# The opening of a two-block transformer kernel: weights of the state-space scan prepared by matrix products, batched transposes, modulation blocks moved

## The reference, cut to what matters

```
h = rmsnorm(x, norm_mix)
dt = exp(log_dt);  ab = exp(lam * dt)                      # complex, per group and state
bb = (ab - 1) / lam * b                                    # complex, (group, state, channel)
bu = einsum('blgh,gph->blgp', h, bb)
xs[t] = ab * xs[t-1] + bu[t]                               # scan over the 256 tokens
y  = Re(einsum('blgp,ghp->blgh', xs, c)) + d_skip * h
a, g = split(gelu(y) @ w_glu);  x = x + a * sigmoid(g)
...
mod = silu(c) @ w_ada + b_ada                              # second block, 1024 -> 6144, two layers
```

## Time and profile before

| what | value |
|---|---|
| median of the runs | 2005.14 us |
| lowest and highest run | 2001.52 and 2005.61 us |
| span of the profiled execution, first to last instruction | 1998.3 us |
| TensorE busy | 1912.5 us (96% of the span) |
| VectorE, ScalarE, GpSimd busy | 934.3, 755.8, 1108.0 us |
| mean granted TensorE clock | 0.979 of full speed |
| first product with `w_glu` starts at | 124.61 us |

### The profile page before, as it was taken

The page is one execution under the profiler, slowest core; times in us unless marked ns, Lnnn a source line. Parts: engine busy times, 40 slices in busy tenths (PEclk is TensorE's granted clock), DMA queues, the critical chain, the costliest instruction groups (busy, mean ns, idle before and its releaser), DMA issues.

```text
span 1998.3 us, 31484 instructions
## 1 busy us (share of the span) xinstructions
PE 1912.5 (96%) x13077; PEld 1644.2 (82%) x13077; DVE 934.3 (47%) x1688; ACT 755.8 (38%) x1212; POOL 1108.0 (55%) x611
## 2 busy tenths in 40 slices
PE   8989999989999999899999999999999999989997
PEld 5578999878887788687778888888788988979997
DVE  7956641364935774732453111114386846372112
ACT  4343553332325422722323222222446435434443
POOL 6435997563535443343443444444468745757885
PEclk8999999989999999999999999999999999989999
DMA  6866776664122132124333323323634421655653
GB/s 165 239 215 225 256 230 219 239 216 156 62 76 64 33 126 64 32 64 137 127 107 126 95 79 121 104 63 110 209 116 128 159 85 54 204 196 174 189 173 98
DMA packets 289490, 276.60 MB, mean 138 GB/s; under 512 B 19802, under 2 KB 276324, under 8 KB 289092
## 3 DMA queue, kind: packets, MB, share of 16 engines
q1 hardware_dynamic: 286804, 271.42, 43.0%
q10 hardware_dynamic: 2192, 2.77, 0.4%
q0 software_dynamic: 352, 0.40, 0.1%
HBM read 266.70 MB, written 4.19 MB: 136 GB/s over the span
## 4 chain that ended last, share of the span: by engine, by line
PE 86%; DVE 6%; ACT 2%; POOL 2%; issue 2%; DMA 1%; SPq 1%; DVEq 0%; ACTq 0%; POOLq 0%
PE gb L2598 19%; PE gb L2599 18%; PE gb L2600 18%; PE gb L1757 3%; PE gb L1755 3%; PE gb L1756 3%; PE gb L1482 3%; PE gb L1483 3%; PE gb L1484 3%; POOL wl L2585 1%; PE mb L1208 1%; PE mb L667 1%; PE gb L667 1%; PE mb L1275 1%; DMA raw<-in_w_ada 1%
## 5 line engine op out<-in xcount | busy, mean ns | idle before, releaser
L2585 POOL TENSOR_TENSOR wl<-raw,wh 128x1024 fp32r<-128x1024 f32 (+3 forms) x448 | 977.8, 2201 | 797.0 <-ACT wh L819 796.7
L819 ACT CAST wh<-raw 128x1024 fp32r<-128x1024 f32 (+3 forms) x452 | 419.4, 937 | 680.8 <-PE gb L2600 399.7
L2598 PE MATMUL gb<-xh,wh 128*128 128x256 f32 (+1 forms) x1856 | 603.4, 325 | 11.0 <-DVE xl L1158 6.9
L2599 PE MATMUL gb<-xl,wh 128*128 128x256 f32 (+1 forms) x1856 | 599.5, 323 | 0.0
L2600 PE MATMUL gb<-xh,wl 128*128 128x256 f32 (+1 forms) x1856 | 599.4, 323 | 0.0
L2598 PEld LDWEIGHTS gb<-xh,wh 128*128 128x128 f32 x1856 | 351.8, 190 | 47.2 <-issue 14.6
L2600 PEld LDWEIGHTS gb<-xh,wl 128*128 128x128 f32 x1856 | 351.8, 190 | 27.6
L2599 PEld LDWEIGHTS gb<-xl,wh 128*128 128x128 f32 x1856 | 351.9, 190 | 27.2
L1755 PE MATMUL gb<-fhh,wh 128*128 128x512 f32 (+1 forms) x352 | 118.4, 336 | 0.0
L1757 PE MATMUL gb<-fhh,wl 128*128 128x512 f32 (+1 forms) x352 | 117.9, 335 | 0.0
L1756 PE MATMUL gb<-fhl,wh 128*128 128x512 f32 (+1 forms) x352 | 117.9, 335 | 0.0
(11 more groups left out here) (475 smaller groups left out, 3028.7 us busy)
## 6 DMA issues: line engine op xcount, KB each, us to landing
raw<-in_w_in SPq DMA_DIRECT2D x62, 1024.0 KB, 5.4
raw<-in_w_ada SPq DMA_DIRECT2D x48, 1024.0 KB, 5.5
raw<-in_w_ffn SPq DMA_DIRECT2D x44, 1024.0 KB, 5.2
raw<-in_mlp_w SPq DMA_DIRECT2D x32, 1024.0 KB, 5.6
raw<-in_w_ffn SPq DMA_DIRECT2D x16, 768.0 KB, 4.3
raw<-in_w_ffn SPq DMA_DIRECT2D x16, 640.0 KB, 4.1
raw<-in_ssm_w_glu SPq DMA_DIRECT2D x8, 1024.0 KB, 6.9
raw<-in_w_out SPq DMA_DIRECT2D x8, 1024.0 KB, 4.8
```

The lines of the kernel that those rows point to most:

```text
L819: nc.scalar.copy(split_half(wh, p, j, h), raw_half(p, it, j, h)).then_inc(hi_ready, 1)
L2585: nc.gpsimd.tensor_tensor(split_half(wl, p, j, h), raw_half(p, it, j, h), split_half(wh, p, j, h).bitcast(F32), ALU.subtract)\
L2598: nc.tensor.matmul(o, H[:, k, :], XH, start=st, stop=False)
L2599: nc.tensor.matmul(o, H[:, k, :], XL, start=False, stop=False)
```

## The change

What it does, by engine:

- Loads. C's real and imaginary parts come by two DMAs (256-byte runs) in place of sixteen; B comes by two DMAs from GpSimd's queue with each pair's 8 KB in one run (`Bq`), in place of four on SyncE's queue and two broadcasts of the gain `norm_mix`; the gain comes as 32 rows (`wq`). SyncE no longer waits for the three lambda loads ahead of its other loads. Some buffers move to other places: x by chunk goes to the ring's slots, so that the first ring load waits for `xg` in place of the transposes of U; the zeros for the Toeplitz matrix wait for these transposes, and the copy of V waits for the zeros.
- B. GpSimd makes diagonal matrices of the gain (`wdiag`); TensorE multiplies B with them (64 products), which transposes it and weights it; VectorE reads the result in PSUM for `Bb`, and its own product with the gain goes.
- C. 32 products with a strided identity take the place of 8 transposes, and come ahead of U. ScalarE copies `Ct` between the fourth and the fifth of its eight `xg` copies.
- x is transposed in two halves through two PSUM banks, after U, then the vectors, `warm(3, 2)`, and only then the two products for `fac`. `warm(21, 3)` becomes `warm(3, 2)`. ScalarE copies all four row-zero parts of F ahead of `fac`.
- V. Transposes, copy and products go by two pairs at a time (16 steps in place of 32). Modulation blocks 0 to 7 stand behind steps 1, 2, 3, 6, 7, 8, 10, 11, blocks 8 and 9 ahead of step 12; k_products(0) stands in step 9, the skip products and k_back(0) in step 11. Behind the last step come k_products(1), block 10, k_back(1), block 11, `warm(8, 1)`. Blocks 12 and 13 stand behind d = 3 and d = 5 of the y loop.
- The ring has 12 modulation blocks, then two `w_glu` blocks, so that the Toeplitz copies (ahead of ring load 12) are issued ahead of the `w_glu` blocks.
- E. GpSimd makes seven halves and the chunk powers in between; VectorE makes one (`e_beside(3, 1)`). `e_last` and `gate_lo` go; GpSimd makes the low parts of the first two `w_glu` blocks.
- The place of U's product with `fac` in VectorE's own order (behind the root, ahead of `f_group(1)`) is the same in both kernels.

The diff, cut to its core:

```diff
-        EARLY_ADA, EARLY_GLU = 10, 2
+        EARLY_ADA, EARLY_GLU = 12, 2
+        K_FIRST = 9
...
             if g == 0:
-                sp.wait_ge(s_U, 1)
+                sp.wait_ge(s_xg, CH)
...
+            for j in range(4):
+                x_by_group(j)
+            act.wait_ge(s_ct5, 1)
+            act.wait_ge(s_vz, 2)
+            nc.scalar.copy(Ct[:, 0, :, 0:GH], gb[:, 1, :].rearrange("p (q h) -> p q h", h=GH)).then_inc(s_Ctc, 1)
+            nc.scalar.mul(Ct[:, 1, :, 0:GH], gb[:, 2, :].rearrange("p (q h) -> p q h", h=GH), -1.0).then_inc(s_Ctc, 1)
+            for j in range(4, CH):
+                x_by_group(j)
...
+            for i in range(2):
+                act.wait_ge(s_xt, i + 1)
+                nc.scalar.copy(x[:, 4 * i:4 * i + 4, 0:SEQ],
+                               gb[:, 1:3, :].rearrange("p b (k t) -> p (b k) t", k=2)).then_inc(s_x1, 1)
...
+            for r in range(4):
+                f_row_zero(r)
+            act.wait_ge(s_fp5, 1)
+            nc.scalar.copy(fac[:, :], gb[:, 1, 0:NCH]).then_inc(s_fac, 1)
...
+            for b in range(PAIRS // 2):
+                act.wait_ge(s_w1t, b + 1)
+                if b >= 2:
+                    act.wait_ge(s_w1u, b - 1)
+                nc.scalar.copy(w1[:, 2 * (b % 2):2 * (b % 2) + 2, :, :],
+                               gb[:, 1 + b % 2, :].rearrange("p (a r m) -> p a r m", a=2, r=2)).then_inc(s_w1, 1)
...
-            warm(21, 3)
+            warm(3, 2)
+            pe.wait_ge(s_Bq, 16 * 2)
+            pe.wait_ge(s_gd, 1)
+            for ri in range(2):
+                for h in range(GH):
+                    for g in range(2):
+                        ins = nc.tensor.matmul(gb[64 * g:64 * g + 64, 3 * ri, PAIRS * h:PAIRS * h + PAIRS],
+                                               Bq[:, ri, g, :, h], wdiag[:, g, h, :], start=True, stop=True)
+            ins.then_inc(s_Bt, 1)
+            pe.wait_ge(s_cnat, 16 * 2)
+            of_parity = ident.rearrange("p (q g h) -> p g q h", q=4, g=2)
+            for ri in range(2):
+                for r in range(8):
+                    for g in range(2):
+                        ins = nc.tensor.matmul(gb[64 * g:64 * g + 64, 1 + ri, 64 * r:64 * r + 64],
+                                               cnat[:, ri, r, :], of_parity[:, g, :, :], start=True, stop=True)
+            ins.then_inc(s_ct5, 1)
...
+            for b in range(PAIRS // 2 + 1):
+                if b == 12:
+                    for n in range(8, 10):
+                        ada_block(pe, n)
+                if b < PAIRS // 2:
+                    w1_transposes(b)
+                if b:
+                    v_products(b - 1)
+                if b in (1, 2, 3, 6, 7, 8, 10, 11):
+                    if b == 1:
+                        pe.wait_ge(s_sc, 1)
+                    ada_block(pe, (1, 2, 3, 6, 7, 8, 10, 11).index(b))
+                if b == K_FIRST:
+                    pe.wait_ge(s_Vc, 2)
+                    k_products(0)
+                if b == K_FIRST + 2:
+                    skip_products()
+                    k_back(0)
+            pe.wait_ge(s_w1, PAIRS // 2)
             k_products(1)
-            ada_block(pe, 5)
...
+            ada_block(pe, 10)
             k_back(1)
-            for n in range(7, EARLY_ADA):
-                ada_block(pe, n)
-            warm(7, 1)
+            ada_block(pe, 11)
+            warm(8, 1)
...
-                late = ((0,), (1,), (), (2,), (), (), (3,), ())[d]
+                late = ((), (), (), (0,), (), (1,), (), ())[d]
...
             dve.wait_ge(s_Ctc, 2)
-            e_beside(2, 1)
-            e_beside(3, 0)
+            e_beside(3, 1)
...
-            e_last(3, 1)
-            dve.sem_inc(s_E, 1)
```

More of the change, by code:

```diff
@@ L712, in _ @@
             sp.dma_start(lnat[:, 0, :], A["ssm_lam_re"][0].rearrange("(q g) p -> q (g p)", g=2)).then_inc(s_lnat, 16)
-            sp.wait_ge(s_lnat, 16 * 3)
             xc = A["x"][0].rearrange("(c j) d -> j c d", j=CH)
[L715 to L721, removed]
+            for ri, name in enumerate(("ssm_c_re", "ssm_c_im")):
+                sp.dma_start(cnat[:, ri, :, :], A[name][0].rearrange("(r g) h p -> (g h) r p", g=8)).then_inc(s_cnat, 16)
             for j in range(CH):
@@ L2336, in _, with x_by_group @@
             act.sem_inc(s_sin, 1)
-            for j in range(CH):
+            def x_by_group(j):
                 if j % 2 == 0:
@@ L2684, in _ @@
             ins.then_inc(s_U, 1)
-            pe.wait_ge(s_x1, 1)
+            pe.wait_ge(s_Ctc, 2)
+            pe.wait_ge(s_xnat, 16)
+            for i in range(2):
+                if i:
+                    pe.wait_ge(s_x1, 1)
+                for k in range(4):
+                    for a in range(2):
+                        ins = nc.tensor.transpose(gb[:, 1 + k // 2, (k % 2) * 256 + a * P:(k % 2) * 256 + a * P + P],
+                                                  xnat[:, a, (4 * i + k) * P:(4 * i + k) * P + P], ident)
+                ins.then_inc(s_xt, 1)
+            pe.wait_ge(s_vnat, 16 * NVEC)
+            pe.wait_ge(s_x1, 2)
+            for a in range(4):
+                ins = nc.tensor.transpose(gb[:, 1, a * P:a * P + P], vnat[:, a, :], ident)
+            ins.then_inc(s_vt, 1)
+            warm(3, 2)
+            pe.wait_ge(s_vc, 1)
+            pe.wait_ge(s_Bb, 1)
             pe.wait_ge(s_small, 32)
@@ L2688, in _ @@
             for a in range(2):
-                ins = nc.tensor.matmul(gb[:, 3, GH * a:GH * a + GH], const[:, REP:CHK], chk[:, a, :], start=True, stop=True)
+                ins = nc.tensor.matmul(gb[:, 1, GH * a:GH * a + GH], const[:, REP:CHK], chk[:, a, :], start=True, stop=True)
             ins.then_inc(s_fp5, 1)
-            pe.wait_ge(s_cnat, 16 * 8)
-            pe.wait_ge(s_gn, 16 * 8)
-            for ri in range(2):
-                for r in range(4):
-                    ins = nc.tensor.transpose(gb[:, 1 + ri, r * P:r * P + P], cnat[:, ri, r, :], ident)
@@ L2696, in _ @@
[L2696 to L2713 removed]
+            pe.wait_ge(s_fac, 1)
@@ new lines, in w1_transposes @@
+            def w1_transposes(b):
+                if b % 4 == 0:
+                    pe.wait_ge(s_F, b // 4 + 1)
+                    pe.wait_ge(s_F0, 2 * (b // 4 + 1))
+                if b >= 2:
+                    pe.wait_ge(s_w1, b - 1)
+                for e in range(2):
+                    q = 2 * b + e
+                    for ri in range(2):
+                        ins = nc.tensor.transpose(gb[:, 1 + b % 2, (2 * e + ri) * P:(2 * e + ri + 1) * P],
+                                                  Fg[q // 8][:, q % 8, ri, :, :], ident)
```

272 lines of the change are left out of this document (104 added, 168 removed).

## The result

| | before | after |
|---|---|---|
| median of the runs | 2005.38 us (2001.52 to 2006.93, 4 runs) | 2014.95 us (2011.33 to 2020.38, 4 runs) |
| ratio, 95% interval | 1 | 1.005 (1.0033 to 1.0068) |
| profiled span | 1998.3 us | 2009.5 us |
| U scaled | 40.8 | 47.2 |
| S starts | 76.6 | 92.2 |

What follows compares the result with a forecast made beforehand. TensorE, busy nearly throughout, bounds the kernel; only the first `w_glu` product's start shifts. U 2.9 us later, S 6.5 later, y 0.9 later, that product 2.6 earlier, plus 0.5 for the clock: -3.1, 2002 us. Range 1997 to 2010.

Steps and rivals of the forecast that it cites:

- B on TensorE: In the front, B's 64 products (128 instructions) take 4.5 us, bounds 3.5 and 11.6, ending at 13.5.
- the wait through ScalarE: In the front, behind C at 17.0, `Ct` copies (1.1) and four `xg` copies (3.8) hold U's transposes until 21.9.
- GpSimd's diagonal product (9.0): In the front, GpSimd's diagonal product, behind six DMA issues and some clears, is ready at 9.0, bounds 8.4 and 12.
- VectorE reaches `Bb` at 14.2: In the front, VectorE reaches `Bb` at 14.2, after B's products end at 13.5, so B's arrival costs nothing.
- V's start: Behind U, steps 0 to 7 and five blocks take 15.0; F(2), ready at 16.3, sets step 8.
- rival (a): Slower rival, low clock in B, C and V's start: U 8 us later, V 2 more, 2010 in all; chance 0.23.
- V's step: In V, a merged step of two pairs takes 1.25 us, bounds 1.15 and 1.46, in place of 1.46.
- What stands among the V products: Between U ready (43.7) and S's start (82.9), steps, blocks, K and skip products and V's copy take 39.1.
- The bound changes sides: Ahead of S, blocks and K products among V's products make TensorE the last instead of VectorE, by 9 us.
- The scan: S's scan on VectorE stays at 19.8 us, ready at 102.7; y starts at 102.8, the Toeplitz copies not last.
- The y loop: From y to the first `w_glu` product, eight steps of 2.4 make 19.2, without the 3.10 block wait, until 122.0.
- the two signs that the prediction named for being wrong: In the opening, S released by VectorE's own E work, or U ready before 40, would show the prediction wrong.

Runs made afterwards that it cites:

- experiment 4: `quiet`: kernel after, with GpSimd's last two clears and the two products of the skip gain moved behind `Bb`; 2016.79 us, ratio 1.0054 to the kernel before.
- experiment 6: `quiet_fac`: kernel of experiment 4 with the products for `fac` right behind U's transposes and their copy ahead of x's copies; 2023.02 us, ratio 1.0100 to the kernel before.
- experiment 1: Kernel after, with the low parts of the first two `w_glu` blocks back on VectorE; 2012.03 us, ratio 1.0039 to the kernel before.
- experiment 7: `fac_warm`: kernel of experiment 6 with three more warm products ahead of U's transposes; 2019.15 us, ratio 1.0078 to the kernel before.
- hold: Experiment 9: kernel of experiment 6 with GpSimd waiting for the end of the root before its E halves; 2013.09 us, ratio 1.0048 to the kernel before.
- fac_warm: The kernel of experiment 7: three more warm products than experiment 6, ahead of U's transposes; 2019.15 us, ratio 1.0078 to the kernel before.
- best2: Kernel `hold` with blocks, K products and ring ordered as before the change, casts ahead of the loop, three E halves on VectorE; 2001.70 us, ratio 0.9977.
- hold_k: The kernel of experiment 12: `hold` with the first K products, the skip products and their copies behind V; 2008.49 us, ratio 1.0003 to the kernel before.
- experiment 5: Kernel after, with `w_glu` loads ahead of the Toeplitz copies and both casts ahead of the gelu loop; 2012.40 us, ratio 1.0043 to the kernel before.
- experiment 12: `hold_k`: kernel `hold` with the first K products, the skip products and their copies behind V; 2008.49 us, ratio 1.0003 to the kernel before.

## Why the prediction was wrong, step by step

- **B on TensorE.** The bound of 5.8 came from the rows nearest to it, and I took 4.5 as if a single stream were faster. It took 7.41 (58 ns each), at no other pace when the clock fell in its midst. With the warm products ending at 9.4 and not 8.4, C ended at 20.4 and not 17.0, and the wait through ScalarE (`Ct`, `xg`), which was sized rightly, passed this on whole: U's transposes ended at 32.4 (28.7), U was ready at 47.2 (43.7). The step that failed is a term mis-sized by 2.9 us; its miss of 3.5 at U is the first of three. B's start, put down to GpSimd's diagonal product (9.0), was set by B's own load (9.82).
- **VectorE reaches `Bb` at 14.2.** Wrong in kind: 25.7. I had put the diagonal product and the clears on GpSimd "behind six DMA issues" and looked only at when they end, not at what they hold up beside them. In the kernel after this costs nothing (experiment 4), but the same effect, E beside the root, took away the gain that an earlier factor could have brought (6 and 9).
- **V's start.** The idle of 2.77 us behind `fac` was seen, its effect on the clock was left to rival (a) with 2 us. The records show 1.2 GHz from 47.0 to 53.8. It cost next to nothing on the path: step 8 began 16.7 us after U was ready, where the forecast has 16.3, because VectorE's F(2) was ready only at 63.6 in any case.
- **V's step.** 1.25 was forecast and 1.18 measured (transposes 0.59, products 0.59): right, on the good side.
- **What stands among the V products.** "The bound changes sides" was right: VectorE waited 14.7 us for V (9 were forecast). From U ready to the start of S it took 45.0, not 39.2. Of these 5.8, 0.4 lie ahead of step 8; 2.5 are the stop inside a modulation block, which the sum did not have, and the rest is the low clock behind that stop (74.3 to 77.7) and from 81.1 to 84.5, where the sum has every step, block and K product at full speed. This is the second miss.
- **The scan.** 19.6, with 19.8 forecast; y followed S by 0.1, and the Toeplitz copies were not last: right.
- **The y loop.** 19.2 was forecast from the loop before; 22.4 was measured. The step said that GpSimd's low parts "run beside the loop", at no cost; three gelu operations took 1.8, 2.8 and 2.3 us in place of 0.4 to 0.8, and TensorE waited 1.96 and 0.60 for the transposes behind them. Taking them off GpSimd gave 1.5 back (experiment 1, in which VectorE had their work to do). This is the third miss, 3.2 us.

So three steps failed: the size of B, the V stretch summed at full speed and without a stop, and GpSimd's low parts put at nothing. 3.5 + 5.8 + 3.2 is 12.5, and the first `w_glu` product came 12.3 later than forecast (134.33 against 122.0). The rival named as slower, (a), had the place of the second miss and part of its cause; its form, B at half clock carrying 8 us to U, did not occur. No rival had GpSimd holding up VectorE. Neither of the two signs that the prediction named for being wrong came (S was released by V's copy, U was not ready before 40); it was wrong by other ways. In the kernel before, GpSimd started E at 41.2, released by the copy of C (`Ct`), which stood behind U there, and it waited for `s_U` too; the root had ended at 32.7, and F's products, which stood beside E, take one operand from PSUM. With C ahead of U and that wait gone, E moved to 21.6, beside VectorE's small operations.

The range ended at 2010 and missed too. It would have had to hold three terms that go wrong together, since all three lie on one chain. And it had no room for how long the low clock lasts behind a stop, which alone moved S by 5 us between experiments 6 and 7.

Open remains what causes the stop of 2.5 us in the middle of a block. It stands at the same place of the program, not of the time: at 71.0 in the kernel after (behind 6 products of the block), and at 65.7 in `hold` (behind 7), whose V began 2.7 us sooner. `fac_warm` shows more: it has three warm products, six matmul instructions, more than `quiet_fac` ahead of this place, and its stop (2.9 us) stands six matmul instructions earlier in the same block, behind 1 in place of 7. So the place goes with the count of instructions, not with what the instruction is. In `best2` and `hold_k`, where other instructions follow V's, stops of 0.34 and 1.43 us lie in the second K products instead. In stretches of 0.2 us, one packet of the instruction queue (0.02 MB) is recorded near the start of the stop in all four of these traces: at 71.0 to 71.2 in the kernel after, at 65.6 to 65.8 in `hold`, at 74.4 to 74.6 in `quiet_fac` (stop from 74.3) and at 75.3 to 75.5 in `fac_warm` (from 74.7). Such packets come every few us elsewhere too. That these are loads of instructions that came late is argued, not shown; nothing was run to take it away. How long the clock stays low behind the stop (3.4 us in the kernel after, 16 in `hold`) is open as well.

## What to carry to other kernels

Before work is moved to GpSimd "beside" VectorE, list VectorE's operations in that stretch by where their inputs lie: small ones with everything in SBUF can wait for GpSimd's whole operation, 2 us for a 0.16 us one, and a chain of them waits again and again. Let GpSimd begin behind such a chain, and lay its work beside operations that take an operand from PSUM. And whatever is put in front of the last product that the next engine waits for (here V's last part, ahead of S) delays that engine by its full length, so only what fills real idle time may stand there. Last, a trace gives one draw of the clock: a stretch behind a stop differed by some 6 us between two traces of the same order.

## What the runs showed of the hardware that I had not expected

- A VectorE operation can stand through several GpSimd operations in a row: one of 128x256 7.08 us beside four low parts (10.18 us), another 7.14 in experiment 5, and in the kernel after one of 128x32 with a single input 4.27 us (from 4.94 to 9.21), through the diagonal product (1.92) and three clears. There the measurement goes beyond the rule quoted above, by which the wait ends with the first operation. In other places one VectorE operation gets in between two of GpSimd's (the root in experiment 6 and the scan in experiment 12: each waits for one).
- The reverse price: GpSimd's E operations took 2.36 and 2.47 us instead of 2.02 in the kernel after while `Bb` was made beside them. On GpSimd's small operations it weighs more: in the kernel before those of 128x128 took 0.77 to 0.90 us beside `Bb`'s of 128x512 (0.81 to 0.93 there; 0.69 in `quiet`, with GpSimd idle), in the kernel after 0.44 to 0.46 with no such neighbour.
- B's 128 products kept one pace at either level of the granted clock, 53 to 56 ns each, with the weight loads (second busy time) filling the whole stretch. The record of 1.00 at the start of a trace is not to be trusted by itself: the first warm products have it too, and their weight loads take 0.34 us as at the low clock. `quiet_fac` settles it. The last weight load of its warm products took 0.21 us, so that its B did start at the full clock. That load, and two stretches of B's line alone, with the granted clock behind the busy times:

```profile
7.42 0.21 PEld L2682 LDWEIGHTS gb<-ones 128*128 128x128 f32 x1 [0.52 <-issue]
```

```profile
9.30:10.80 1.50, 1.50 (x28) 1.50 (x28) 1.00 0.95 156
11.00:16.00 5.00, 5.00 (x94) 5.00 (x92) 0.50 1.02 248
```

So the clock was not what made B long, and my doubling of 5.8 in the bounds and in rival (a) had no ground. V's products, with weights as wide and as many moving columns, did follow the clock: 16 took 0.59 us at 2.4 GHz (37 ns each) and 1.00 at 1.2. They have 128 rows and B's have 32, and B's weights are read in strides; which of this sets B's pace was not tried.
